# Three projections by row tiles over weight halves, four conditioning chunks on VectorE, cross-attention in four parts

## The reference, cut to what matters

```python
for l in range(DEPTH):            # DEPTH = 2
    mix = hybrid_mixer(h, ...)    # ends in merged @ w_out
    h = layer_norm(ALPHA * h + mix, ln1_g[l], ln1_b[l])
    h = layer_norm(ALPHA * h + cross_attention(h, mem, cq_w[l], ckv_w[l], co_w[l]), ln2_g[l], ln2_b[l])
    h = layer_norm(ALPHA * h + swiglu(h, ffn_wi[l], ffn_wo[l]), ln3_g[l], ln3_b[l])

def cross_attention(u, mem, cq_w, ckv_w, co_w):    # 4 heads of 256
    q = (u @ cq_w)...; k, v = split(mem @ ckv_w)
    return softmax(q @ k.T / 16) @ v @ co_w

def second_block(x, c, ctx, c_ctx, w_ada, b_ada, ...):
    sh_a, sc_a, g_a, sh_f, sc_f, g_f = split(silu(c) @ w_ada + b_ada, 6)       # w_ada: 1024 x 6144
    csh_a, csc_a, ... = split(silu(c_ctx) @ w_ada + b_ada, 6)                  # its first two parts are used
    ...                                            # attention, gating, 16 experts
```

## Time and profile before

| what | value |
|---|---|
| median of 3 runs | 1613.58 us (1608.23 to 1618.84) |
| the profiled execution | 1610.38 us, span 1608.6 us |
| around the span | 1.8 us |
| instructions in the span | 20461 |
| TensorE, share of the span | 97% |
| VectorE, ScalarE, GpSimd | 71%, 56%, 5% |
| mean granted TensorE clock | 0.991 |

### The profile page before, as it was taken

How to read it: one execution, slowest core, us unless ns; L and a number is a source line. 1 busy time by engine, 2 the same in 40 slices (tenths; PEclk the granted TensorE clock), 3 DMA queues, 4 the chain that set the end, 5 groups by cost and what they waited for, 6 DMA issues and landing times.

```text
span 1608.6 us, 20461 instructions
## 1 busy us (share of the span) xinstructions
PE 1562.3 (97%) x8144; PEld 1294.3 (80%) x8144; DVE 1146.5 (71%) x1615; ACT 902.3 (56%) x1377; POOL 79.7 (5%) x75
## 2 busy tenths in 40 slices
PE   9999999999999999999999999999989989999997
PEld 9988887786888799879887778888767877888785
DVE  7457856656555583677566588766666689999998
ACT  5467644435444354865435355543454568888885
POOL 0010000000000000100000000000200000000005
PEclk9999999999999999999999999999999899999999
DMA  7545335427555354543446288864450329999994
GB/s 296 187 156 199 117 131 209 184 105 289 203 187 184 131 212 182 199 168 132 151 163 236 79 320 322 313 247 158 157 177 31 132 81 367 370 378 370 376 368 171
DMA packets 52201, 339.35 MB, mean 211 GB/s; under 512 B 7835, under 2 KB 8477, under 8 KB 13316
## 3 DMA queue, kind: packets, MB, share of 16 engines
q1 hardware_dynamic: 48932, 331.79, 55.5%
q0 software_dynamic: 3168, 6.20, 1.1%
HBM read 332.82 MB, written 10.49 MB: 213 GB/s over the span
## 4 chain that ended last, share of the span: by engine, by line
PE 81%; DVE 11%; ACT 3%; DMA 2%; issue 1%; POOL 1%; SPq 0%; DVEq 0%; ACTq 0%
PE bank L736 23%; PE bank L738 22%; PE bank L737 22%; PE bank L742 4%; DVE wls L2088 4%; DMA raw<-in_ws_dram 2%; PE bank L804 2%; PE bank L870 2%; DVE h L2058 1%; ACT whs L1470 1%; PE bank L990 1%; POOL sm L3036 1%; DVE sm L2070 1%; PE bank L970 1%; ACT arena L1456 1%
## 5 line engine op out<-in xcount | busy, mean ns | idle before, releaser
L2088 DVE TENSOR_TENSOR wls<-raw,whs 128x1024 fp32r<-128x1024 f32 x442 | 524.8, 1226 | 198.0 <-ACT whs L1470 196.9
L1470 ACT ACTIVATE whs<-raw 128x1024 fp32r<-128x1024 f32 x442 | 445.0, 1052 | 232.8 <-PE bank L738 159.8
L736 PE MATMUL bank<-whs,P1h 128*128 128x512 f32 (+1 forms) x732 | 289.7, 396 | 3.7 <-issue 2.1
L738 PE MATMUL bank<-whs,P1l 128*128 128x512 f32 (+1 forms) x732 | 284.3, 388 | 0.0
L737 PE MATMUL bank<-wls,P1h 128*128 128x512 f32 (+1 forms) x732 | 283.6, 387 | 0.0
L736 PE MATMUL bank<-whs,P0h 128*128 128x512 f32 (+1 forms) x640 | 256.3, 400 | 2.5 <-DVE P0l L2058 1.2
L738 PE MATMUL bank<-whs,P0l 128*128 128x512 f32 (+1 forms) x640 | 249.3, 390 | 0.0
L737 PE MATMUL bank<-wls,P0h 128*128 128x512 f32 (+1 forms) x640 | 249.2, 389 | 0.0
L736 PEld LDWEIGHTS bank<-whs,P1h 128*128 128x128 f32 x732 | 137.6, 188 | 32.5 <-issue 4.5
L738 PEld LDWEIGHTS bank<-whs,P1l 128*128 128x128 f32 x732 | 137.4, 188 | 28.9
L737 PEld LDWEIGHTS bank<-wls,P1h 128*128 128x128 f32 x732 | 137.7, 188 | 26.7
(11 more groups left out here) (282 smaller groups left out, 2450.4 us busy)
## 6 DMA issues: line engine op xcount, KB each, us to landing
raw<-in_ws_dram SPq DMA_DIRECT2D x264, 1024.0 KB, 4.9
landing<-in_ws_dram SPq DMA_DIRECT2D x38, 1024.0 KB, 6.5
lnb<-in_ln_g_dram SPq DMA_DIRECT2D x6, 512.0 KB, 5.7
lnb<-in_ln_b_dram SPq DMA_DIRECT2D x6, 512.0 KB, 6.5
ydram<-arena POOLq DMA_DIRECT2D x4, 512.0 KB, 12.3
mid<-in_bias_dram SPq DMA_DIRECT2D x1, 2048.0 KB, 9.7
h<-in_x_dram SPq DMA_DIRECT2D x2, 512.0 KB, 3.8
lnb<-in_mem_dram SPq DMA_DIRECT2D x1, 1024.0 KB, 13.7
```

Source lines behind the costliest of these rows:

```text
L736: e.matmul(out, x[0], w[0], start=start, stop=False, skip_group_check=skip)
L738: return e.matmul(out, x[1], w[0], start=False, stop=stop, skip_group_check=skip)
L1470: e.activation(hi, src, ACT.Copy, bias=0.0, scale=1.0).then_inc(*high.done(n, f))
L2088: e.tensor_tensor(lo, src, f32(hi), ALU.subtract).then_inc(*low.done(n, f))
```

## The change

What it does:

1. `w_out` and `co_w` are planned by row halves (`by_rows`) and run by the new `gemm_tiles` in the order `OUT_SEQ` of (unit, tile). Tile 0 is complete after step 5 of 8, and three steps of tile 1 follow. Tile 0 is turned after the first quarter of step 7.
2. `cq_w` keeps its plan, but is run by `gemm_tiles` in the order `IN_SEQ`, with tokens on partitions. Its first three steps are of tile 0, and tile 1 is turned after three quarters of step 2. The query rows are copied out (`qr`) and turned into columns by four groups of four transposes.
3. The first two chunks of the MLP are led by `lead_chunks` with the same idea: steps (chunk, unit, tile) 000, 010, 100, 001, 011, 110, 101, 111, and the hidden columns of chunk 0 are turned after the seventh.
4. `norm_turn` remains after the third norm of layer 0 alone. Chunk 2 is made there on TensorE. Chunks 0, 1, 3 are summed on VectorE in the MLP of layer 0, for both vectors, and chunk 6 with the others in layer 1. The gain and bias on `h` are done tile by tile after steps 4 and 5 of `cq_w` and of the lead (`norm_rows`).
5. Cross-attention is done in four parts (tile, head pair), with a table `links` that says after which tick each link of each part is put. The scale of the softmax moves from VectorE to ScalarE. The product with v has 128 columns instead of 256.
6. A fourth slot of high and low parts, `mid_pair`, is open from step 2 of `w_out` to the start of the MLP.

The diff, cut to its core:

```diff
-BY_PE = ((0, 1, 2), (3, 6))
-BY_DVE = ((), (7, 8, 9, 4, 5, 10, 11))
+BY_PE = 2
+BY_DVE = ((0, 1, 3), (7, 8, 9, 4, 5, 10, 11, 6))
+OUT_SEQ = ((0, 0), (1, 0), (0, 1), (2, 0), (3, 0), (1, 1), (2, 1), (3, 1))
+IN_SEQ = ((0, 0), (1, 0), (2, 0), (0, 1), (1, 1), (3, 0), (2, 1), (3, 1))
...
+    def gemm_tiles(self, name, seq, half_of_unit, part=None, evac=None, at=None, fine=False):
...
+        for j, (u, t) in enumerate(seq):
+            if u not in units:
+                units[u] = self.take(name)
...
+            for kk in range(4):
+                if part:
+                    part(units[u], u, kk, t, opens and kk == 0, closes and kk == 3)
+                if fine and kk == 1:
+                    self.tick()
+                if (j, kk) in at:
+                    at[j, kk]()
+            if closes and evac:
+                evac(half[j], t)
+            if all(v != u for v, _ in seq[j + 1:]):
+                self.release(units[u])
+            self.tick()
+            if (j, 4) in at:
+                at[j, 4]()
...
+        def lead_chunks():
+            units = {}
+            steps = ((0, 0, 0), (0, 1, 0), (1, 0, 0), (0, 0, 1), (0, 1, 1), (1, 1, 0), (1, 0, 1), (1, 1, 1))
...
+                if (c, u, t) == (1, 0, 1):
+                    turn(0)
+                if t:
+                    self.release(units[c, u])
...
+        links = {5: [("tq", 0)], 6: [("sc", 0)], 7: [("ex", 0)], 8: [("nz", 0)], 9: [("tp", 0)], 10: [("w", 0)],
+                 11: [("o", 0), ("tq", 1)], 12: [("sc", 1)], 13: [("tq", 2), ("ex", 1)], 14: [("sc", 2), ("nz", 1)],
+                 15: [("tp", 1), ("ex", 2)], 16: [("w", 1), ("nz", 2)], 17: [("o", 1), ("tq", 3), ("tp", 2)],
...
             def cross(l):
...
+                linked(W, {"tq": turn_q, "sc": scores, "tp": turn_p, "w": weigh})
+                W.gemm_tiles("cq_w", IN_SEQ, IN_AT[0], tiles_part(...),
+                    at={(0, 4): lambda: W.feed(1), (1, 0): lambda: W.feed(1), (1, 2): second_turn, (2, 4): free}, fine=True)
...
+                W.gemm_tiles("co_w", OUT_SEQ, OUT_AT[0], tiles_part(...),
+                    at={(2, 4): hold, (6, 0): first_turn, (7, 4): lambda: W.feed(1)}, fine=True)
...
             def cond_half(n, f):
...
+                    for i in range(1 + early):
+                        o, by = sums(c, i), cs[:, 2 * k + i:2 * k + i + 1]
...
+                    for f in between or ():     # VectorE, in ln_half of tile 1: low part of tile 0, half a split
+                        f()
                     ve.wait_ge(pool, "pow", l, which, t)
...
+                lead = {(0, 4): lambda: W.feed(1), (1, 0): lambda: W.feed(1), (1, 2): second_turn, (2, 4): free,
+                        (3, 4): lambda: norm_rows(l, 2, 0), (4, 4): lambda: norm_rows(l, 2, 1)}
```

More of the change, by code:

```diff
@@ L1128, in down_part @@
                     mm.here("B", l, c)
[L1130 removed]
+                lead = {(0, 4): lambda: W.feed(1), (1, 0): lambda: W.feed(1), (1, 2): second_turn, (2, 4): free}
+                W.mlp(nch, up, down, held, turn_hidden, up_part, None, down_part, held and lead)
                 mm.here("mlp_end", l)
```

565 lines of the change are left out of this document (323 added, 242 removed), and 2 rows, old and new, of the table links.

## The result

| | before | after |
|---|---|---|
| median of 7 runs each | 1614.25 us (1608.23 to 1618.84) | 1623.28 us (1621.73 to 1626.32) |
| ratio to before, 95% interval | | 1.0065 (1.0044 to 1.0086) |
| span of the profiled execution | 1608.6 us | 1624.5 us |
| mean granted clock of TensorE | 0.991 | 0.977 |

The changed kernel is 0.65% slower, 9.0 us by the medians. The forecast was 1628 us, with its own range 1617 to 1640.

A forecast was written before the change was run, and what follows sets the result against it. TensorE was taken as the bound, busy 1562.3 of 1608.6 us. 1610.4 - 19.5 (work) - 10.4 (waits that go) + 43.2 (waits that come) + 4.1 (clock) = 1627.8, forecast as 1628 us, own range 1617 to 1640.

The forecast's parts named there:

- Work, -19.5: TensorE, both layers: work lost and gained, mainly four conditioning chunks leaving (-28.2) against added small products and turns; sum -19.5 us.
- Waits that go, -10.4: TensorE's waits in `w_out` (2.0 for both layers) and cross-attention (8.3) disappear: -10.4 us.
- Waits that come, +43.2: New TensorE waits at norms, cross-attention and the MLP's start: 21.6 us per layer, 43.2 for both.
- first turns of tiles 0 and 1: Turns behind two norms per layer: tile 0 late by 1.1 us in all, tile 1 by 0.8.
- part 2: Cross-attention: softmax chain of query part 2 waits for step 8's split, then ScalarE and VectorE; TensorE waits 2.3 us per layer.
- hidden turn: Start of the MLP: turn of hidden columns waits for VectorE's low parts, sums, gain and bias; 5.4 us per layer.
- before `down 0`: Start of the MLP: another split, tile 1's gain and bias, a product and the low part cost 2.8 us more per layer.
- The clock, +4.1: TensorE's granted clock falls after one in five of twelve long new waits, 1.7 us each: +4.1 us.
- Rival C: TensorE's clock falls after all twelve long waits in cross-attention and the MLP's start: 20.4 instead of 4.1, 1644 us; chance 0.14.
- A: New waits are about half the sum, since splits are done ahead: 1603 us, range 1592 to 1612; chance 0.23.
- B: Nearly all new waits are covered and the change does what its shape says: 1585 us; chance 0.11.
- Edits at nothing: VectorE's added sums, some 40 us, hide beside MLP matmuls past the start; the fourth slot costs nothing.

The follow-up runs named there:

- x_cols: Changed kernel with the 48 one-column records at the start of layer 1 issued in three groups of 16 between groups of 24 wide products: 1620.47 us, ratio 1.0034.
- x_nz: Changed kernel with reciprocal and scale of the softmax weights in the same step as their exponential, ahead of the weight split: 1610.77 us, ratio 0.9982.
- x_lead: Changed kernel with conditioning sums begun one chunk later and gain and bias behind the products hid of chunk 0 at the MLP's start: 1609.98 us, ratio 0.997.
- x_rows: Changed kernel with only VectorE's gain and bias at the MLP's start moved behind the products hid, conditioning sums left in place: 1621.31 us, ratio 1.0051.
- x_warm: Changed kernel with unused products of a constant put in on TensorE ahead of the long waits, in both layers: 1620.20 us, ratio 1.0026.
- x_all: Changed kernel with x_lead, x_cols, x_nz with part 0's chain two half steps later, context squares four steps later, gain and bias behind reciprocals: 1584.40 us, ratio 0.981.
- x_bare: Kernel before with conditioning products at norms 1 and 2 of both layers cut from 16 wide records to two wide and six of two columns: 1607.22 us, ratio 0.9947.
- x_all3: x_all with part 2's product with v half a step later and the last block's 32 one-column records in two groups of 16: 1582.30 us, ratio 0.9789.

## Why the prediction was right, step by step

**The total** was 4.7 us too high (1628 against 1623.3), within its own range. As a change it fits less well: +17.4 on the profiled execution before was forecast, the medians give +9.0, and the profiled pair, against which the terms are held here, +15.9. The kernel before was measured 3.9 us above the execution from which the sum starts, and that hides part of the miss. The work and the waits that go hold. Of the other two terms one was too high and the other too low by about the same.

**Work, -19.5:** by the sums above -22.3, in the later kernels about -20.5. The largest term, 28.2 for the four chunks, stands: 16 records are left. Two prices were a little high. The new 128-column products of a group of 16 start 0.111 us apart at full clock (342.66, 1.95 us for 16 in the changed kernel), where 0.125 was taken, so the +1.5 for the product with v was about nothing. The one-column records start 0.106 apart (x_cols), where 0.114 was taken from a row's whole time, which includes the end of its last record. The figure of 25 ns that the Trainium skill has in "TensorE: Matmul & The Clock Gate", section "Wait — 56ns, not 53.3ns?", did not decide here: a group of 16 took 1.84 us, over four times as long, and the measurement decides.

**Waits that go, -10.4:** gone, all of them.

**Waits that come, +43.2:** 29.6 are listed, link by link:

| link, per layer | forecast | layer 0 | layer 1 |
|---|---|---|---|
| first turns of tiles 0 and 1 (1.1 + 0.8) | 1.9 | 0 | 0 |
| query part 0 | 2.7 | 2.31 | 2.28 |
| softmax weights, part 0 | 3.6 | 3.26 | 3.26 |
| part 1 | 2.9 | 2.31 | 2.31 |
| part 2 | 2.3 | 0.42 | 0.32 |
| hidden turn | 5.4 | 4.27 | 5.71 |
| before `down 0` | 2.8 | 0 | 0.58 |
| second unit of the MLP | none | 0 | 2.61 |

The first turns are covered, with no wait listed. The places and the releasers of the four largest are those forecast, and x_nz, x_lead and x_rows show their causes: each wait goes when what stood ahead on the waiting engine is moved. The sums cost less than 0.75 each: 4.94 for the first eight halves in layer 0 (0.88 + 4.06). Part 2 came out small for two reasons: its exponential stood ahead of the split, not behind (ScalarE 332.57, split 334.54), so only reciprocal and scale came after, and the slow clock filled 1.0 of it, since it is 1.45 in x_lead. The wait before `down 0` was there, but under the slow clock: x_warm brought it out with 2.23 us. These two places make some 4.4 of the 13.6 us between 43.2 and 29.6. The wait of 2.61 in layer 1 I had missed: two squares of the context rows, 2.24 us, stand ahead of the split on ScalarE.

**The clock, +4.1:** this step failed. I took one fall in five waits from the row before, where four of five waits had none. Here seven of nine long waits had one (half of those in cross-attention over the other profiles), and a row of one-column products lowered the clock with no wait at all. By the sums it is +19.5 in the profiled pair, nearer +10 in the typical execution by the estimate above. Rival C had the mechanism, only too often, and its price of 1.7 per fall is about right (5 x 0.34 at 865, 895 and 940); its clock term of 20.4 is close to the pair's. It came out too high in all because it was added to the 43.2 of waits, of which 29.6 came, partly since falls fill them.

So forecast and result agree partly by luck: against the profiled pair the idle time was 14 us too high (+32.8 against +18.7), and the clock 15 us too low. **Rivals A and B** had too few waits; A's half of 43.2 would have been 21.6, and 29.6 came. What B describes, nearly all new waits covered at 1585, took the edits of x_all: 1584.4. That B named the same figure is chance, since its 5 us were not added up.

**Edits at nothing:** held. Past the MLP's start no wait for VectorE is listed in its chunks, so the sums are hidden there. At the start, where the forecast counted them, they are the larger part of the wait: x_lead lies 11.3 us under x_rows. They could have been hidden there too, by one chunk's delay. The fourth slot was not tried by itself.

The Trainium skill, "TensorE: Matmul & The Clock Gate", section "Why this matters for your kernels", says that idle gaps between bursts bring back the slow clock. This case's runs agree in so far as five of seven falls went with filling products in the gaps (x_warm). They differ in that the longer wait was not the surer one (a fall behind 2.28 and none behind 3.26 in the changed kernel), and that a row of one-column products brought a fall with no gap; there the measurement decides.

## What to carry to other kernels

When work is taken off the engine that is the bound, ask what it covered: here at least two thirds of a chunk's price came back as waits for the norm (x_bare). If the new order interleaves chains of three engines, list what stands ahead of each link on the engines that serve in order, and put links (reciprocal, scale, product) ahead of bulk work (weight splits, sums, gain and bias) at every place where the bound engine waits: eight moves in the order without any change of the work gave 2.6%. Don't price waits and clock as a sum. Filling the gaps to hold the clock up gave 3 to 6 us here, and taking the waits away 42, since then both go.

## What was not expected of the hardware

- In and behind a row of 48 records of one-column products (some 5.1 us at full clock, by the groups of x_cols) the granted clock fell in all seven profiles, to 0.50 over 5 us in five of them, at a cost of 1.7 to 5.1 us, although TensorE shows as fully busy; in groups of 16 with 24 wide products between them it stayed at 1.00 (x_cols).
- Falls are not tied to the longest waits: behind both waits of 3.26 us the clock stayed at 1.00 in the changed kernel, behind 2.3 us it fell to 0.66 to 0.76, and in x_lead there was a fall behind the 3.26 too (0.75 and 0.57 at 310 and 315), and none behind the 2.31 that follows. So something besides the length of the wait decides; what it is is left open.
- The fall behind the second row of one-column products stayed when the row was divided (x_all3), so a group of 16 records with turns and waits of 0.31 and 0.74 us behind it is enough there. Which of them does it is left open.
